# Squares of the SSD output on ScalarE and VectorE, S5 loads behind the sample states, and S5 steps set later in a one-core decoder layer

## The reference

```
h = rms_norm(x);  proj = h @ w_in        # z | x,B,C | dt | u | gate_a | gate_b
xs, bm, cm = silu(causal_conv(xbc))      # 8 groups of 8 heads, state 128
y = ssd(xs, dt, a, bm, cm, state_ssm)    # branch A, group by group
y = (y + xs * d_ssm) * silu(z)           # the gated SSD output, 4096 features
y_a = rms_norm(y, norm_ssm) @ w_ssm_out  # needs the sum of y*y over the features
s   = s5_scan(u, lambda, b, state_s5)    # branch B, a complex diagonal state
y_b = glu(gelu(Re(C s) + D u) @ w_glu)
merged = sigmoid(gate_a) * y_a + sigmoid(gate_b) * y_b
x = x + rms_norm(merged @ w_out)
x = x + rms_norm(swiglu(rms_norm(x)))
```

## Time and profile before

| | |
|---|---|
| runs | 2634.53, 2640.14, 2636.06 us |
| median | 2636.06 us |
| the profiled execution | 2637.47 us |
| its span in the profile | 2635.7 us |
| mean granted TensorE clock | 0.983 of full speed |
| TensorE matmuls busy | 2527.9 us (96%) |
| VectorE busy | 1684.8 us (64%) |
| ScalarE busy | 1114.4 us (42%) |
| GpSimd busy | 67.4 us (3%) |

### The profile page before, as it was taken

How to read it: one execution, slowest core, us unless ns; L and a number is a source line. 1 busy time by engine, 2 the same in 40 slices (tenths; PEclk the granted TensorE clock), 3 DMA queues, 4 the chain that set the end, 5 groups by cost and what they waited for, 6 DMA issues and landing times.

```text
span 2635.7 us, 53075 instructions
## 1 busy us (share of the span) xinstructions
PE 2527.9 (96%) x19434; PEld 2457.4 (93%) x19434; DVE 1684.8 (64%) x3144; ACT 1114.4 (42%) x1761; POOL 67.4 (3%) x81
## 2 busy tenths in 40 slices
PE   5999999999999999999999999979999999999996
PEld 4989999999999989999999999969999999999996
DVE  4768778786887867668886666574544554544444
ACT  4544535444453534454425333343333443333332
POOL 1000000000000001100000000000000000000000
PEclk9999999999999999999999999989999999999998
DMA  5665657666565668544456776555555555565552
GB/s 149 181 188 171 189 156 213 181 183 191 171 183 170 211 155 232 158 119 135 151 156 199 199 202 188 168 157 165 169 166 163 166 159 166 167 199 166 166 164 73
DMA packets 656789, 450.96 MB, mean 171 GB/s; under 512 B 71160, under 2 KB 647944, under 8 KB 655648
## 3 DMA queue, kind: packets, MB, share of 16 engines
q1 hardware_dynamic: 636480, 433.44, 55.9%
q10 hardware_dynamic: 20128, 15.15, 1.9%
HBM read 409.35 MB, written 39.12 MB: 170 GB/s over the span
## 4 chain that ended last, share of the span: by engine, by line
PE 85%; DVE 9%; issue 3%; ACT 1%; DMA 1%; SPq 0%; ACTq 0%; DVEq 0%
PE acc L1924 26%; PE acc L1925 25%; PE acc L1926 25%; PE side L1911 2%; DVE abc L1322 2%; DVE w_lo L1243 2%; PE side L2241 1%; PE side L2007 1%; PE side L2090 1%; ACT w_hi L773 1%; PE side L2276 1%; PE side L2277 1%; DVE cacc L1286 1%; PE side L2261 1%; PE side L2080 1%
## 5 line engine op out<-in xcount | busy, mean ns | idle before, releaser
L1243 DVE TENSOR_TENSOR w_lo<-raw,w_hi 128x1024 fp32r<-128x1024 f32 (+2 forms) x692 | 846.2, 1228 | 709.3 <-ACT w_hi L773 704.1
L773 ACT ACTIVATE w_hi<-raw 128x1024 fp32r<-128x1024 f32 (+2 forms) x692 | 721.6, 1046 | 1061.8 <-PE acc L1926 1022.8
L1924 PE MATMUL acc<-h_hi,w_hi 128*128 128x288 f32 x3472 | 1056.1, 304 | 14.4 <-DVE w_lo L1243 7.8
L1926 PE MATMUL acc<-h_hi,w_lo 128*128 128x288 f32 x3472 | 1029.8, 297 | 0.0
L1925 PE MATMUL acc<-h_lo,w_hi 128*128 128x288 f32 x3472 | 1028.8, 296 | 0.0
L1924 PEld LDWEIGHTS acc<-h_hi,w_hi 128*128 128x128 f32 x3472 | 659.2, 190 | 33.2 <-issue 24.2
L1925 PEld LDWEIGHTS acc<-h_lo,w_hi 128*128 128x128 f32 x3472 | 658.8, 190 | 0.3
L1926 PEld LDWEIGHTS acc<-h_hi,w_lo 128*128 128x128 f32 x3472 | 657.8, 189 | 0.0
L1924 PE MATMUL acc<-f_hi,w_hi 128*128 128x288 f32 x704 | 208.7, 296 | 0.0
L1926 PE MATMUL acc<-f_hi,w_lo 128*128 128x288 f32 x704 | 207.5, 295 | 0.0
L1925 PE MATMUL acc<-f_lo,w_hi 128*128 128x288 f32 x704 | 207.2, 294 | 0.0
(11 more groups left out here) (345 smaller groups left out, 2898.4 us busy)
## 6 DMA issues: line engine op xcount, KB each, us to landing
raw<-in_w_in_dram SPq DMA_DIRECT2D x512, 256.0 KB, 3.2
raw<-in_w_ffn_up_dram SPq DMA_DIRECT2D x352, 256.0 KB, 3.3
raw<-in_w_ffn_down_dram SPq DMA_DIRECT2D x160, 256.0 KB, 3.0
raw<-in_w_ssm_out_dram SPq DMA_DIRECT2D x128, 256.0 KB, 3.3
raw<-in_w_glu_dram SPq DMA_DIRECT2D x128, 256.0 KB, 3.6
h<-in_state_ssm_dram SPq DMA_DIRECT2D x64, 256.0 KB, 4.2
out_ssm_sample_dram<-h SPq DMA_DIRECT2D x64, 256.0 KB, 2.9
raw<-in_w_out_dram SPq DMA_DIRECT2D x64, 256.0 KB, 3.0
```

Of the source, the lines that this page charges most:

```text
L773: copy = lambda out, in_, **k: nc.scalar.activation(out, in_, ACT.Copy, **k)
L1243: tt(w_lo[:, slot, 0:n], raw[:, slot, 0:n], w_hi[:, slot, 0:n].bitcast(F32), ALU.subtract).then_inc(lo_ready, 1)
L1924: mm(o_, wh, xh[:, kt, :], start=first and i == 0, stop=False)
L1926: done = mm(o_, wl, xh[:, kt, :], start=False, stop=last and i == n - 1)
```

## The change

It has five parts.

- The squares are one `Square` activation on ScalarE at t = 27. VectorE adds them a group later (t = 8; those of the last group at z = 1): halves onto each other, then quarters, then into `sst`. GpSimd does none of it. `y_summed` now counts three per group.
- `b_load` and `c_load` go from t = 18 to 25 to t = 24 to 27 (real parts) and z = 0 to 3 (imaginary parts); `s5_states_load` goes to z = 4 and 5. What reads them follows: `c_turns` (TensorE) from t = 24, 26 to 27, 30, the states' turn from 29 to 32, the products with B on VectorE from t = 27, 28, 29 to 31, 32, 33. `sum_squares` and `norm` go two steps on.
- `T0` is 33 instead of 31; `skip_added` stands four and two steps ahead of it (z = 29, 31 instead of 29, 30).
- `FIN0` is 76 instead of 72: the turns of the final states come four steps later, `finals` on VectorE stay where they are. The gelu steps 4 to 7, `v_round` and `v_remainder` go one or two steps on.
- `o_matrices(1, ...)` goes from z = 43, 49 to 39, 45 and the first three `u2_load` from z = 10, 12, 19 to 12, 14, 20.

```diff
-T0 = SCAN0 + 3
+T0 = SCAN0 + 5
 OUT0 = SCAN0 + 31
-FIN0 = OUT0 + 13
+FIN0 = OUT0 + 17
...
-    return {66: 0, 67: 1, 69: 2, 70: 3, 71: 4, 72: 5, 74: 6, 75: 7}.get(z, -1)
+    return {66: 0, 67: 1, 69: 2, 70: 3, 72: 4, 73: 5, 75: 6, 76: 7}.get(z, -1)
...
                 sp.wait_ge(sem("y2_ready"), NG)
+                wait(sp, "c_landed", 32 * k)
...
-                if t in (26, 27):
-                    s5_states_load(t - 26)
-                if 18 <= t < 22:
-                    b_load((t - 18) // 2, t % 2)
-                if 22 <= t < 26:
-                    c_load((t - 22) // 2, t % 2)
+                if t in (24, 26):
+                    b_load(0, (t - 24) // 2)
+                if t in (25, 27):
+                    c_load(0, (t - 25) // 2)
...
+                if z in (0, 2):
+                    b_load(1, z // 2)
+                if z in (1, 3):
+                    c_load(1, z // 2)
+                if z in (4, 5):
+                    s5_states_load(z - 4)
...
-            squares(0)
-            with pool.Fori(1, NG) as g:
-                squares(g)
...
+                    if t == 27:
+                        act.wait_ge(sem("y_split"), g * 4 + 4)
+                        nc.scalar.activation(yb[:, :, :], yb[:, :, :], ACT.Square).then_inc(sem("y_squared"), 1)
...
+            def squares_added(g):
+
+                dve.wait_ge(sem("y_squared"), g + 1)
+                tt(yb[:, 0:2, :], yb[:, 0:2, :], yb[:, 2:4, :], ALU.add).then_inc(sem("y_summed"), 1)
+                dve.wait_ge(sem("y_summed"), g * 3 + 1)
+                tt(yb[:, 0, :], yb[:, 0, :], yb[:, 1, :], ALU.add).then_inc(sem("y_summed"), 1)
+                dve.wait_ge(sem("y_summed"), g * 3 + 2)
+                tt(sst[:, :], sst[:, :], yb[:, 0, :], ALU.add).then_inc(sem("y_summed"), 1)
...
-                if z in (T0 - 2, T0 - 1):
-                    skip_added(z - T0 + 2)
+                if z in (T0 - 4, T0 - 2):
+                    skip_added((z - T0 + 4) // 2)
```

More of the change, by code:

```diff
@@ L620, in _ @@
                     load(c, c // 4, kc, rows(w_in, kc)[:, :, OFF_GA + k * 256:OFF_GA + (k + 1) * 256])
-                for q, first in enumerate((10, 12, 19, 28)):
+                if z in (0, 2):
[4 more added lines that the diff above has]
+                    s5_states_load(z - 4)
+                for q, first in enumerate((12, 14, 20, 28)):
                     if z in (first, first + 1):
@@ L727, in _ @@
             pool.memset(sst[:, :], 0.0).then_inc(made, 1)
[L729 to L736, removed]
             pool.memset(cm[:, :, :], 0.0).then_inc(made, 1)
@@ L1003, in s5_parameters @@
                     nc.scalar.activation(pr5[:, 8, :], pr5[:, 6, :], ACT.Sin, scale=-1.0, bias=eps1[:, 2:3]).then_inc(sem("s5_sin"), 1)
-                if t in (25, 27):
-                    c_copies((t - 25) // 2)
-                if t == 30:
+                if t in (28, 31):
+                    c_copies((t - 28) // 3)
+                if t == 33:
                     act.wait_ge(*reach("s5_states_turned", 2))
@@ L1039, in inputs_copy @@
                 if i == 0 and m == 0:
-                    act.wait_ge(sem("y_summed"), 4 * NG)
+                    act.wait_ge(sem("y_summed"), 3 * NG)
                     groups_stored(act)
@@ L1118, in _ @@
                     ya_store(z - 2)
-                if z == 5:
+                if z == 7:
                     norm(1, 1.0 / D_INNER, 1)
@@ L1144, in _ @@
                     gelu_square(gelu_at(z))
-                if OUT0 + 12 <= z < OUT0 + 20:
-                    v_round(z - OUT0 - 12)
+                if OUT0 + 14 <= z < OUT0 + 22:
+                    v_round(z - OUT0 - 14)
                 if FIN0 < z <= FIN0 + 5:
@@ L1345, in side_work @@
                 if ssd:
+                    if t == 8 and not (isinstance(g, int) and g == 0):
+                        squares_added(g - 1)
                     if t == 0:
@@ L1391, in side_work @@
                         dve.wait_ge(sem("y0_ready"), g + 1)
-                        wait(dve, "y_summed", g * 4)
+                        wait(dve, "y_summed", g * 3)
                         skip(0, s2, g, par)
@@ L1594, in s5_parameters @@
                 qr, qi = bc(pr(12), S5C, 2), bc(pr(13), S5C, 2)
-                if t == 27:
+                if t == 31:
                     dve.wait_ge(*reach("b_landed", 64))
@@ L1598, in s5_parameters @@
                     link(tt(t1, bi, qi, ALU.mult))
-                if t == 28:
+                if t == 32:
                     link(tt(t2, br, qi, ALU.mult))
                     link(tt(br, t0, t1, ALU.subtract))
-                if t == 29:
+                if t == 33:
                     link(tt(t0, bi, qr, ALU.mult))
@@ L1754, in _ @@
                 s5_parameters(28 + z)
-                if z == 6:
+                if z == 1:
+                    squares_added(NG - 1)
+                if z == 8:
                     norm(1)
@@ L1765, in _ @@
                     responses_copy(i)
-                if z in (T0 - 2, T0 - 1):
-                    skip_added(z - T0 + 2)
-                if z in (T0 + 12, T0 + 18):
-                    o_matrices(1, (z - T0 - 12) // 6)
+                if z in (T0 - 4, T0 - 2):
+                    skip_added((z - T0 + 4) // 2)
+                if z in (T0 + 6, T0 + 12):
+                    o_matrices(1, (z - T0 - 6) // 6)
                 if out_block(z - 1) >= 0:
@@ L1783, in _ @@
                     dve.drain().then_inc(sem("s5_scanned"), 1)
-                if OUT0 + 12 <= z < OUT0 + 20:
-                    v_remainder(z - OUT0 - 12)
+                if OUT0 + 14 <= z < OUT0 + 22:
+                    v_remainder(z - OUT0 - 14)
             def glu(k, b, q):
@@ L2161, in s5_parameters @@
                     last.then_inc(sem("lam_turned"), 1)
-                if t == 24:
-                    pe.wait_ge(*reach("c_landed", 64))
+                if t == 27:
+                    pe.wait_ge(*reach("c_landed", 32))
                     pe.wait_ge(sem("h0_updated"), 8 * NG)
@@ L2166, in s5_parameters @@
                     c_turns(0)
-                if t == 26:
+                if t == 30:
                     pe.wait_ge(sem("c_ready"), 2)
+                    pe.wait_ge(*reach("c_landed", 64))
                     c_turns(1)
-                if t == 29:
+                if t == 32:
                     pe.wait_ge(sem("s5_states_landed"), 64)
@@ L2176, in s5_parameters @@
                         last.then_inc(sem("s5_states_turned"), 1)
-                if t == 32:
+                if t == 34:
                     pe.wait_ge(*reach("s5_states_ready", 2))
-                    pe.wait_ge(sem("y_summed"), 4 * NG)
+                    pe.wait_ge(sem("y_summed"), 3 * NG)
                     sum_squares()
```

## The result

The changed kernel takes 2604.46 us (median of four runs, 2602.76 to 2607.78), against 2635.3 for the kernel before in its four runs. The ratio is 0.9884 with a 95% interval of 0.987 to 0.9898: 30.6 us less (27 to 34). The forecast was 38.4 less, so the direction is right, the range holds the time, and the gain falls 8 us short. The profiled execution took 2607.8 us, with a span of 2605.9: the longest of the four, 3.3 above their median, where the one of before lay 2.2 above its own.

What follows compares the result with a forecast made beforehand. TensorE, busy 96% of the span, was taken as the bound, so only its waits count. Terms 18.0 + 6.0 + 2.2 + 6.7 + 5.5 = 38.4 us off the profiled 2637.5, and 1.4 for the median, gave 2597.5 us (2587 to 2614).

Steps and rivals of the forecast that it cites:

- A, the squares: Group ends: TensorE's seven waits for zs go, Square and additions stay hidden; gain 18.0 us (12.6 to 18.0).
- The rival that the squaring of `yb` itself slows VectorE: Group ends: Square on ScalarE slows the clamp just so, the 24.0 us don't come; 2621.5 us, chance 5%.
- the slower case: Group ends: Square delays exponential and split, VectorE's additions delay step 8's split; +14.0 us, 2650, chance 3%.
- late next at the boundary is TensorE itself: Group boundary: once the zs waits go, TensorE is the next to be late, with 1.5 us to spare.
- a sign of being wrong: Group period staying near 113 us without a wait would mean the loop's own issue was hidden under it.
- B, the clock: Group ends: without the waits, four low-clock stretches of TensorE at 1.5 us go; gain 6.0, least 3.0.
- C, the loads: Group 7 and tail: h waits and low clock go (7.9 us), a weight shortage comes; net 2.2 (-0.8 to 7.9).
- absorbs about half: z = 0 to 5: raw slots three chunks ahead absorb half of 6 us shortage; new wait 3.0, low clock 2.7.
- The rival that the queue has room: S5 loads behind the weights cost nothing, their gain is 7.9 us, the sum 44.1, time 2592; chance 20%.
- D, the first T block: First t_shift: wait falls from 4.0 to about 1.1 us, st wait and low clock go; gain 6.7 (4.1 to 7.8).
- E, the final states: Chunks 72 to 74: of the 5.3 us wait 1.8 stays on w_lo, clock gives 2.0; gain 5.5 (3.3 to 7.3).
- The rival that VectorE bounds the S5 steps anyway: S5 steps: VectorE stays the bound, T block gives 4.1 and final states 3.3 us; sum 33.6, 2602.5, chance 20%.

Runs made afterwards that it cites:

- e5: Kernel before, GpSimd keeping the squares but starting them only after TensorE's last chunk of the group: 2615.44 us, ratio 0.9931.
- e1: Kernel before with only the squares moved to ScalarE and VectorE: 2613.8 us, ratio 0.9921.
- e2: Kernel before with only the S5 loads and their readers moved: 2632.67 us, ratio 0.9994.
- e4: Changed kernel with the S5 loads and their readers back at their old places: 2602.9 us, ratio 0.9879.
- e11: Changed kernel with skip_added back in the two steps right ahead of the first T block: 2607.01 us, ratio 0.9896.
- e9: Changed kernel with VectorE's final states set ahead of the gelu of the same step: 2598.13 us, ratio 0.9861.
- e7: Changed kernel with the S5 loads of B and C spread over more steps: 2598.61 us, ratio 0.9873.
- e6: Changed kernel with TensorE's loop over groups 1 to 6 written out: 2598.64 us, ratio 0.9872.
- e10: Changed kernel with the edits of e6, e7 and e9 together: 2591.65 us, ratio 0.9841.

## Why the prediction was right or wrong

**A, the squares: right.** The seven waits went. The timelines of VectorE and ScalarE in the changed kernel show the price and the place that the forecast named:

```profile
324.57 1.22 DVE L1237 TENSOR_TENSOR w_lo<-raw,w_hi 128x1024 fp32r<-128x1024 f32 x1
325.70 1.25 DVE L1316 TENSOR_SCALAR abc<-abc,gtv 32x32 f32<-32x32 f32 x8
...
327.24 1.21 DVE L1237 TENSOR_TENSOR w_lo<-raw,w_hi 128x1024 fp32r<-128x1024 f32 x1
```

```profile
326.83 1.15 ACT L887 ACTIVATE yb<-yb 128x1152 f32<-128x1152 f32 x1
327.89 0.40 ACT L847 ACTIVATE abc<-abc 32x256 f32<-32x256 f32 x1
```

The Square takes 1.15 (forecast 1.2), and the exponential follows it with ScalarE idle 0.77 afterwards. VectorE's three additions take 0.75, 0.46 and 0.46 (forecast 1.65 in all), and it still idles 1.5 us behind them. The rival that the squaring of `yb` itself slows VectorE is refuted: the split at 327.24, over half of it beside the Square, takes 1.21. So is the slower case: the Square starts at 326.83 and is done before TensorE begins the next group at 328.85. What failed is the sentence that late next at the boundary is TensorE itself, with 1.5 us to spare: its passage from one loop pass to the next, 1.8 to 1.9 us here, lay under two of the seven waits. The forecast names it only as a sign of being wrong, and as a microsecond in the lower end of its range; in the sum it had no term, and it cost 3.7 us.

**B, the clock: half right.** 6.0 was forecast on the ground that the waits cause the stretches. They went with the waits, but in the profiled execution of the change the two loop passages have such stretches of their own (3.0). The forecast held that waits up to 1.2 don't lower the clock and took 1.8 to be as harmless; in the changed kernel those of 1.77, 1.92 and 1.82 all did, in e5 those of 1.72 and 1.81 at the same places did not. Over the profiles of the change and the experiments 5 of 16 passages have such a stretch behind them, and 3 of 7 waits for `w_lo` at the final states (1.8 to 1.9 us, one of them 2.25). So whether such a wait costs 1.5 more is partly chance, and this part of the miss is one execution's. A and B together: 24.0 forecast, 20.1 in the trace, 20.8 in e1.

**C, the loads: the mechanism right in kind, the term too small.** The extra DMA work was sized well: 22.5 us of all engines forecast, and the packets of B, C and the states took 23.5. The step that failed is that the ring "absorbs about half", with a new wait of 3.0 and 2.7 of low clock: 5.7 were forecast and 9.6 were lost. The wait grew by 6.3 (1.5 to 7.8), and the low clock with it is 10.2 us long, of which some 4.6 fall beside work. What was gained ahead of z = 1 came out at 9.6 instead of 7.9, so that the sum is 0.0 instead of 2.2. What the forecast did not look at is SP's own timeline of the kernel before, where weight issues behind B take 3.4 and 5.9 us. The two weight pairs behind imaginary B loads hold SP for 5.6 + 7.8 = 13.4 us in the change, more than the three chunks of lead (3 x 3.2 = 9.6). The rival that the queue has room (C = 7.9) is refuted by e2 and e4. The new wait of SP on `c_landed` cost nothing: the first imaginary C load is issued at 991.41 us, right after a weight, and both real ones had landed by 988.2.

The page of the Trainium skill that spoke for that rival (DMA: Bandwidth & Descriptors, "Why small descriptors are slow (HBM only)") gives a packet a fixed few cycles on top of its 32-byte beats, which makes a 64-byte run an estimated 2.3 times as dear per byte as a 1-KB one. In the DMA records of the changed kernel's trace a 64-byte packet takes 14.0 ns on average, and a 1-KB packet 58.1 in the same stretch (970 to 1010 us), which is 3.9 times per byte. The measurement decides: by the page's figure the forecast put the S5 loads at about 14 us, and their packets took the 23.5. B's 16384 packets make 14.4 us of all 16 engines, C and the states 9.1.

**D, the first T block: right.** 1.1 us of wait forecast, 1.15 measured; 0.6 stayed on `st`, where none was forecast; the low clock went. 5.9 of 6.7. e11 confirms the 1.1, but not how it was told: two chunks gained and 0.3 lost on each VectorE step would leave no wait of 4.0. `gs` comes one VectorE step of 3.5 later, which leaves 4.0 + 3.5 - 6.4.

**E, the final states: the wait right, the clock not.** The forecast named chunk 74, `w_lo` and 1.8 us of wait, and 1.82 is there. The 2.0 us for the clock came only by a quarter, since the wait of 1.8 again lowered it for 3.4 us (1.5). 4.0 of 5.5. The lower bound of 3.3 has no working; with the wait as forecast and no gain from the clock it would be 3.5. The rival that VectorE bounds the S5 steps anyway is half true: the order of its queue did it, not its work, as e9 shows.

The gain in the traces (30.7 us) is 7.7 short of the forecast: 3.7 for the loop's passages, 4.5 for low clock behind three waits of 1.8, 2.2 for the loads and 0.8 in D make 11.2, and 3.5 the other way lie in small differences ahead of 908 us (2.8) and behind z = 84 (0.7), where nothing in the change accounts for them. Of these the 3.7 and the 2.2 have a cause that the experiments show, the 0.8 is read from the trace alone, and the 4.5 of low clock are partly chance, as said under B.

## What to carry to other kernels

A wait that is removed uncovers what lay under it at the same place: before counting its full length, look for a loop edge, a queue or a slower engine that would have been late there a little less. When work slows its neighbour, moving it in time can be worth as much as giving it to another engine, as e5 shows with one line. Of a transfer in short runs count the packets and read how long the issue right behind it holds its queue; two such transfers within the lead of the ring made it run dry here, and spread out (e7) the wait was gone, at the price of 3.2 us at h.

## What was not expected of the hardware

- TensorE's passage from one loop pass to the next costs 1.3 to 1.9 us where the pass is two groups long (some 225 us), and shows no wait when the loop is written out (e6, e10). In the traces of before its place was under the `zs` wait.
- Waits of TensorE as short as 1.8 us were followed by 3.4 us at the lower of its clock levels in the changed kernel, at three places. Over the profiles of the change and the experiments the same waits often were not: 5 of 16 at the loop's passages were, 3 of 7 at the final states. One profile is not enough to price it.
- A pair of weight DMAs behind a B load of 4096 packets holds the issuing SP for 3.1 to 7.8 us in the two kernels, against 1.1 to 1.5 us for the pairs behind C loads in the changed one.
- A VectorE split that began beside GpSimd's squaring ended 1.08 us after the squaring did, in 16 cases of 16 (before and e5), whether it had begun 0.1 or 1.2 us behind it: it stood still for the rest of GpSimd's instruction.
